# Gate and up products of experts 1 to 15 as couples of 64-row tiles, two weight pairs held at a time

## The reference

```
gate, idx = lax.top_k(aff.T, cap)                  # cap = 64 tokens of each sequence
xs = xf[idx]                                       # (16 experts, 64, 1024)
hid = jax.nn.silu(jnp.einsum('ecd,edf->ecf', xs, w_gate)) * jnp.einsum('ecd,edf->ecf', xs, w_up)
out = jnp.einsum('ecf,efd->ecd', hid, w_down) * gate[..., None]
y = zeros.at[idx.reshape(-1)].add(out.reshape(-1, D))
```

## Time and profile before

| | us |
|---|---|
| median of three runs (1526.59 to 1527.58) | 1526.74 |
| span of the profiled execution | 1525.3 |
| TensorE products busy in it | 1511.1 |
| TensorE weight loads busy in it | 1222.7 |
| VectorE busy | 1312.2 |
| ScalarE busy | 1215.8 |
| GpSimd busy | 333.7 |
| mean traffic with HBM | 324 GB/s |

### The profile page before, as it was taken

The page is one execution under the profiler, slowest core; times in us unless marked ns, Lnnn a source line. Parts: engine busy times, 40 slices in busy tenths (PEclk is TensorE's granted clock), DMA queues, the critical chain, the costliest instruction groups (busy, mean ns, idle before and its releaser), DMA issues.

```text
span 1525.3 us, 22267 instructions
## 1 busy us (share of the span) xinstructions
PE 1511.1 (99%) x7854; PEld 1222.7 (80%) x7854; DVE 1312.2 (86%) x1415; ACT 1215.8 (80%) x1435; POOL 333.7 (22%) x154
## 2 busy tenths in 40 slices
PE   9999999999999999999999999999999999999997
PEld 7888878888873787888888888888888888888886
DVE  7684786685766799999999999999999999999988
ACT  6453556344454689999999999999999999999997
POOL 0000001000012232242322423233242322420103
PEclk9999999999999999999999999999999999999999
DMA  9533547333476999999999999999999999999998
GB/s 347 182 136 127 159 139 278 109 125 98 138 240 224 395 420 395 405 394 415 398 404 403 398 408 391 399 406 406 404 393 408 399 402 403 397 411 386 391 387 353
DMA packets 156407, 498.60 MB, mean 327 GB/s; under 512 B 10880, under 2 KB 36608, under 8 KB 156352
## 3 DMA queue, kind: packets, MB, share of 16 engines
q1 hardware_dynamic: 144624, 461.54, 77.3%
q0 software_dynamic: 9280, 31.07, 6.7%
q10 hardware_dynamic: 2448, 5.25, 1.3%
HBM read 473.70 MB, written 20.97 MB: 324 GB/s over the span
## 4 chain that ended last, share of the span: by engine, by line
PE 92%; ACT 3%; DVE 2%; DMA 1%; issue 1%; SPq 0%; POOLq 0%; POOL 0%; DVEq 0%; ACTq 0%
PE ps L2063 78%; PE ps L2111 4%; PE ps L2118 2%; PE ps L2222 2%; PE ps L2162 1%; ACT w_high L1229 1%; PE ps L2380 1%; PE ps L2168 1%; DVE w_rest L1380 1%; DMA u_rows<-arena 1%; ACT arena L1200 1%; DMA raw<-w_qkv 1%; PE ps L2662 0%; PE ps L2376 0%; PE ps L2398 0%
## 5 line engine op out<-in xcount | busy, mean ns | idle before, releaser
L1380 DVE TENSOR_TENSOR w_rest<-raw,w_high 128x2048 fp32r<-128x2048 f32 x212 | 478.0, 2283 | 42.3 <-ACT w_high L1229 25.2
L1229 ACT CAST w_high<-raw 128x2048 fp32r<-128x2048 f32 x184 | 352.1, 1915 | 17.3 <-PE ps L2063 14.3
L2063 PE MATMUL ps<-w_high,xt_high 128*128 128x512 f32 x984 | 304.9, 390 | 2.3 <-DVE ht_rest L1896 1.8
L2063 PE MATMUL ps<-w_rest,xt_high 128*128 128x512 f32 x984 | 304.3, 389 | 0.0
L2063 PE MATMUL ps<-w_high,xt_rest 128*128 128x512 f32 x984 | 304.3, 389 | 0.0
L2063 PEld LDWEIGHTS ps<-w_high,xt_high 128*128 128x128 f32 x984 | 184.4, 188 | 42.6 <-issue 3.0
L1380 DVE TENSOR_TENSOR w_rest<-early,w_high 128x2048 fp32r<-128x2048 f32 x90 | 204.4, 2286 | 13.7 <-ACT w_high L1229 13.7
L2063 PEld LDWEIGHTS ps<-w_high,xt_rest 128*128 128x128 f32 x984 | 184.7, 188 | 38.4
L2063 PEld LDWEIGHTS ps<-w_rest,xt_high 128*128 128x128 f32 x984 | 184.7, 188 | 38.3
L1380 DVE TENSOR_TENSOR w_rest<-raw_more,w_high 128x2048 fp32r<-128x2048 f32 x92 | 206.0, 2273 | 5.4 <-ACT w_high L1229 5.4
L1200 ACT COPY arena<-arena 32x256 f32<-32x256 f32 x464 | 187.4, 404 | 10.8
(11 more groups left out here) (317 smaller groups left out, 2278.2 us busy)
## 6 DMA issues: line engine op xcount, KB each, us to landing
raw<-w_down SPq DMA_DIRECT2D x64, 1024.0 KB, 8.5
raw<-w_gate SPq DMA_DIRECT2D x62, 1024.0 KB, 8.6
raw<-w_up SPq DMA_DIRECT2D x62, 1024.0 KB, 8.9
raw_more<-w_down SPq DMA_DIRECT2D x32, 1024.0 KB
early<-w_down SPq DMA_DIRECT2D x32, 1024.0 KB, 7.9
raw_more<-w_gate SPq DMA_DIRECT2D x31, 1024.0 KB
raw_more<-w_up SPq DMA_DIRECT2D x31, 1024.0 KB
early<-w_gate SPq DMA_DIRECT2D x31, 1024.0 KB, 9.2
```

What stands on the lines that cost most here:

```text
L1229: nc.scalar.copy(w_high[:, i % SLOTS, :], src).then_inc(high_done, 1)
L1380: nc.vector.tensor_tensor(w_rest[:, j, :], src, w_high[:, j, :].bitcast(F32), ALU.subtract).then_inc(rest_done, 1)
L2063: done = nc.tensor.matmul(out, lhs, rhs, start=start and part == 0, stop=stop and part == 2)
```

## The change

In `gate_up` each product over 128 rows becomes two products over 64 rows, one on partitions 0 to 63 and one on 64 to 127, issued one behind the other. Such a couple works on two weight pairs at a time, the gate pair and the up pair of the same features (a group; a call has four). The six steps of a run are three parts times two chunks. In run 0 the lower rows take the gate pair into bank 0 and the upper rows the up pair into bank 2; run 1 does the same for banks 1 and 3; in runs 2 and 3 the roles are swapped (lower rows up, upper rows gate), so that each bank gets both halves of the rows. TensorE waits for its own earlier runs (`run_done`, new, and `pair_used`) so that the two tiles never write one bank at once. `pair_used` is raised by two at the end of the fourth run. Both pairs' `rest_done`, and all waits for the banks, now stand ahead of the group. The number of columns that stream is the same per couple as per product before (512), and the number of products is doubled. The semaphore `k_high` is merged into `q_high`. The queues of ScalarE, VectorE, SyncE and GpSimd for the experts are unchanged.

```
--- before.py
+++ after.py
@@ -162,6 +162,8 @@
 THIRD_BANKS = (5, 7)
 FOURTH_BANKS = (6, 7)
 LIST_BANKS = (4, 6)
+RUNS = 4
+SIGNALS = RUNS - 1
 TABLE_BANKS = ((4, 4), (6, 4))
 ROW_BANKS = (4, 6)
 
@@ -324,7 +326,6 @@
         wq_in = [sem(f"wq_in{part}") for part in range(Q_PARTS - 1)]
         wk_in = sem("wk_in")
         q_high, q_rest = sem("q_high"), sem("q_rest")
-        k_high = sem("k_high")
         diag_done = sem("diag_done")
         rstd_mm = sem("rstd_mm")
         rstd_t_done = sem("rstd_t_done")
@@ -412,6 +413,7 @@
         third_silu_done, third_hid_done = sem("third_silu_done"), sem("third_hid_done")
         first_xt_done = sem("first_xt_done")
         xt_mm, xth_done, xtr_done = sem("xt_mm"), sem("xth_done"), sem("xtr_done")
+        run_done = sem("run_done")
         silu_done, hid_done = sem("silu_done"), sem("hid_done")
         ht_mm, hth_done, htr_done = sem("ht_mm"), sem("hth_done"), sem("htr_done")
         last_in = sem("last_in")
@@ -1107,7 +1109,7 @@
                 act.wait_ge(xt_in[kc], 16)
                 nc.scalar.activation(ut_high[:, kc * T:(kc + 1) * T], xt_raw[:, kc, :], ACT.Copy,
                                      scale=g_col[:, kc:kc + 1]).then_inc(uth_done, 1)
-            first_high(1, 0, K_PARTS, wk_in, k_high)
+            first_high(1, 0, K_PARTS, wk_in, q_high)
             first_high(1, 1, K_PARTS, raw_in[1], high_done)
             x_squares(0)
             first_root(0)
@@ -1789,7 +1791,7 @@
                     else:
                         first_rest(0, part, Q_PARTS, high_done, 1, rest_done)
                 split_x(0, kc, kc + 1)
-            first_rest(1, 0, K_PARTS, k_high, 1, q_rest)
+            first_rest(1, 0, K_PARTS, q_high, Q_PARTS, q_rest)
             first_rest(1, 1, K_PARTS, high_done, 2, rest_done)
             for i in (1, 3):
                 x_squares(i)
@@ -2537,18 +2539,38 @@
                 pe.wait_ge(route_done, TRUNKS + QUARTERS)
                 nc.tensor.matmul(pieces, same_lane[:, :], spread_rows[:, :, :].rearrange("p t n -> p (t n)"), start=True, stop=True).then_inc(route_mm, 1)
 
-            def gate_up(e, lo, *banks_free):
-                for i in range(GU_PAIRS):
-                    if i < len(banks_free):
-                        pe.wait_ge(*banks_free[i])
-                    j = (lo + i) % SLOTS
-                    pe.wait_ge(rest_done, SLOTS * body_q(e, lo + i) + j + 1)
-                    for k in range(2):
-                        kc = 2 * (i // 2) + k
-                        at = slice(kc * P, (kc + 1) * P)
-                        last = products([(bank(2 * (i % 2) + n), xt_high[:, at], xt_rest[:, at], *w(j, k * HALF + n * BANK, BANK),
-                                          kc == 0, kc == KC - 1) for n in range(2)])
-                    last.then_inc(pair_used, 1)
+            def run(runs):
+
+                lower, upper = slice(0, P // 2), slice(P // 2, P)
+                for step in range(2 * 3):
+                    for on, (out, what, column, pair, first, last, kc_first) in ((lower, runs[0]), (upper, runs[1])):
+                        k, part = step // 3, step % 3
+                        at, cols = slice((kc_first + k) * P, (kc_first + k + 1) * P), slice(k * HALF + column, k * HALF + column + BANK)
+                        x = xt_rest if part == 2 else xt_high
+                        weights = w_rest if part == 1 else w_high
+                        mm = nc.tensor.matmul(out, x[on, at], weights[on, pair, cols], start=first and step == 0, stop=last and step == 5)
+                return mm
+
+            def gate_up(e, lo, number, *banks_free):
+
+                for wait in banks_free:
+                    pe.wait_ge(*wait)
+                for i in range(0, GU_PAIRS, 2):
+                    for ii in (i, i + 1):
+                        pe.wait_ge(rest_done, SLOTS * body_q(e, lo + ii) + (lo + ii) % SLOTS + 1)
+                    slots = [(lo + i) % SLOTS, (lo + i + 1) % SLOTS]
+                    for r in range(RUNS):
+                        before = SIGNALS * (GU_PAIRS // 2 * number + i // 2)
+                        if r >= 2:
+                            pe.wait_ge(run_done, before + r - 1)
+                        elif r and i:
+                            pe.wait_ge(pair_used, pairs_before(e) + lo + i)
+                        elif i:
+                            pe.wait_ge(run_done, before)
+                        what, n, opened = r // 2, r % 2, r < 2
+                        last = run([(bank(2 * of + n), of, n * BANK, slots[of], i == 0 and opened, i == GU_PAIRS - 2 and not opened, i)
+                                       for of in (what, 1 - what)])
+                        last.then_inc(*((run_done, 1) if r < SIGNALS else (pair_used, 2)))
 
             def down(s, h, e, lo, first=0, end=D_PAIRS, lhs=None):
 
@@ -2622,26 +2644,26 @@
             pe.wait_ge(ys_done, 1)
             down(0, 0, 0, 8, 0, 2)
             first_hidden_t(1, 6)
-            gate_up(0, 10, (xtr_done, 3))
+            gate_up(0, 10, 0, (xtr_done, 3))
             down(0, 0, 0, 16, 2, 3)
-            gate_up(0, 19, (silu_done, 3), (hid_done, 3))
+            gate_up(0, 19, 1, (silu_done, 3), (hid_done, 3))
             down(0, 0, 0, 24, 3, 4)
             down(1, 1, 0, 28)
             products_read(1)
             with pe.Fori(1, E - 2) as f:
-                gate_up(f, 8, (xtr_done, f + 3), (htr_done, 2 * f + 1))
+                gate_up(f, 8, 2 * f, (xtr_done, f + 3), (htr_done, 2 * f + 1))
                 pe.wait_ge(ys_done, f + 1)
                 down(2 * f, 0, f, 16, 0, 1)
-                gate_up(f, 17, (silu_done, 2 * f + 3), (hid_done, 2 * f + 3))
+                gate_up(f, 17, 2 * f + 1, (silu_done, 2 * f + 3), (hid_done, 2 * f + 3))
                 down(2 * f, 0, f, 24, 1, 4)
                 products_read(f + 1)
                 down(2 * f + 1, 1, f, 28)
-            gate_up(E - 2, 8, (xtr_done, E + 1), (htr_done, 2 * E - 3))
+            gate_up(E - 2, 8, 2 * E - 4, (xtr_done, E + 1), (htr_done, 2 * E - 3))
             pe.wait_ge(ys_done, E - 1)
             down(2 * E - 4, 0, E - 2, 16)
             down(2 * E - 3, 1, E - 2, 20)
             pe.wait_ge(hid_done, 2 * E - 1)
-            gate_up(E - 1, 0)
+            gate_up(E - 1, 0, 2 * E - 3)
             pe.wait_ge(ys_done, E)
             down(2 * E - 2, 0, E - 1, 8, 0, 2)
             pe.wait_ge(hid_done, 2 * E)
```

## The result

The changed kernel takes 1732.34 us (median of four runs, 1727.13 to 1733.40) against 1526.66 us before: 1.134 times as long, with a 95% interval of 1.1327 to 1.1353. The profiled execution has a span of 1731.6 us, 206.3 more than before. The forecast was 1708, with 1660 to 1760 around it.

A forecast was written before the change was run, and what follows sets the result against it. TensorE was taken as the bound, with ScalarE and VectorE within 4%. Thirteen repetitions at 12.3 us more plus 21.6 elsewhere gave 182 us, on the 1525.3 span 1707, so 1708 us as median; range 1660 to 1760.

The forecast's parts named there:

- The bound: Expert loop: TensorE sets the time, 65.28 us a repetition; ScalarE busy 63.1 us and VectorE 62.6 us of it.
- The term that decides: Holding two weight pairs per group: refill path 7.1 us, cover 5.4 us; repetition 77.6 us against 65.3.
- The eight waits: TensorE waits in one loop repetition, followed through three engine queues: 0.1 to 2.9 us each, 11.4 in all.
- Expert 0's part: The two calls of expert 0, by the same reckoning as the loop: 10.9 us more.
- The couples: gate_up's 64-row product pairs: 224 ns instead of 226.6, 2880 couples, minus 7 us, ends 0 and minus 31.
- The lower end, 216 ns: Fastest spacing allowed for a couple of 512 columns, from the kernel's last sixteen products; sum 172 us instead of 182.
- Tiles in and out: Entering and leaving 64-row tiles in each call: 0.1 us in, 0.23 out, 10 us for 30 calls.
- The clock: Rival: 1.2 GHz for the group behind the 2.6 and 2.9 us waits, 150 us in all, 1860; chance 0.06.
- a sign of being wrong: Listed for the loop: granted clock below 1.00, a repetition under 66 us, or couples at 453 ns.
- the filling is hidden: Rival: couples win and the casts and subtractions for a group hide under the other group, 1505 us; chance 0.05.
- couples run in sequence: Rival: 512-column couples do not run together, 453 ns each, 653 us more, 2180; chance 0.02.
- the waits are half of what was reckoned: Rival: queued work catches up, so the waits cost 91 us, 1560 to 1660; chance 0.06.

The follow-up runs named there:

- hold_full: The changed kernel with each couple replaced by one product over 128 rows, waits and release kept; 1748.42 us, 1.144 times before.
- swap_full: swap_tiles with full-height products in the same order, waits and releases; 1585.20 us, 1.0378 times before.
- need_rel: The kernel before, no tiles, with weight pairs both needed in twos and given back in twos, bank waits unchanged; 1717.93 us, ratio 1.1247.
- narrow: The kernel before with gate_up products over 256 columns instead of 512, twice as many; 1563.35 us, ratio 1.0239.
- swap_tiles: The changed kernel with each couple on one weight pair, banks exchanged two runs later, pairs held for less; 1586.02 us, ratio 1.038.
- need_only: The kernel before, no tiles, with TensorE waiting for both pairs of a group ahead of the first; 1569.39 us, ratio 1.0280.
- keep_clock_10: The changed kernel with 10 products of 128 columns into an unused bank ahead of each call's opening waits; 1723.65 us, ratio 1.1296.

## Why the prediction was right, and where it was off

**The bound.** "TensorE sets the time and two engines are within 4% of doing so" was right, and so was what followed: the time came back as idle time on three engines, with the busy time of ScalarE and VectorE unchanged. TensorE's span less its busy time grew by 150 us (164.4 against 14.2), as forecast.

**The term that decides: right.** Path 7.1 us against a cover of 5.4: the rows bear it out (7.0 from the first cast on, where the prediction has 6.9), and hold_full, swap_full and need_rel show the same cause without tiles. The repetition was put at 77.6 and took 78.4; 12.3 us more against 13.1. Of the 0.8 that are missing, 0.5 are the couples (192 at 226.6 instead of 224 ns). The eight waits came to 11.4 us by the reckoning (its entries add up to 11.5) and to 10.4 in the brackets, which count from modelled ends; from one start to the next each of the seven is some 0.16 longer (a last product's end, 0.39 behind its start, lies that much behind the next start), 11.5 in all. Single ones are off by up to 0.5, either way, and it is in part luck that they cancel. Expert 0's part was put at 10.9 and took 14.4, with low clock in it; expert 14's at 5.6 and took 4.2; the end at 3.7 and took 3.4.

**The couples: size wrong.** I took 224 ns from the scores and got 226.6, the upper end. The step that failed is reading 10 ns above streaming in the scores (248 columns, 64 rows) as something that 64-row tiles bring. The narrow products show a fixed 13.3 at full height; why the scores have only 10 there stays open. The lower end, 216 ns, was the spacing of plain float32 products of 256 columns, another kind of product, and no run shows it for a couple. The term is 0 and not minus 7 us. The rule of the Trainium skill (TensorE: Matmul & The Clock Gate, Part 3, "The mechanism"), by which a load hides only behind products of another row group, would have made this the place of a gain. Before and after, loads of 188 and 189 ns disappear in a spacing of 227 ns, to the same rows and to others, so the trace does not bear it out for these products. The other page of the Trainium skill (TensorEngine Tiling (Array Packing), "The Problem"), that tiles are for contractions of 64 or less, agrees with the runs.

**Tiles in and out: right in size, wrong in place.** 0.33 us a call was in the sum, 10 us for 30 calls. On the way out it is to be seen behind the last couple of a call:

```profile
854.11 0.40 PE L2551 MATMUL ps<-w_high,xt_rest 64*128 64x512 f32 x2
854.44 0.73 PE L2065 MATMUL ps<-w_high,ht_high 128*128 128x512 f32 x2
855.01 0.62 PE L2065 MATMUL ps<-w_rest,ht_high 128*128 128x512 f32 x2
```

The starts are 0.33 and then 0.57 us (for two products) apart, where a spacing of 227 ns gives 0.23 and 0.45: 0.22 us a call, as reckoned. On the way in TensorE waits in the loop anyway. And yet swap_tiles and swap_full differ by 0.8 us, and the ordinary repetitions of hold_full and of the changed kernel are both 78.4 us: the next wait takes it up. "Where TensorE waits on entering anyway, less" was the right half of the sentence.

**The clock: a rival that came true in part.** I gave 0.06 to a fall behind both long waits of every repetition, 150 us. It came in 4 of 13 repetitions, for 3.7 us each in those that can be compared. A granted clock below 1.00 in the loop was named as a sign of being wrong, and that sign came: 0.94 in those repetitions. It does not touch the reckoning of the waits, which holds in the nine others. The row I held against it, a wait of 1.82 us without a fall, was shorter than the 2.9 in question, and a single one; waits of 1.86 to 1.91 us had no fall in most repetitions of need_only and keep_clock_10 and had one in others, so one row could not settle it. It should have been a term of the sum with ends 0 and 48 us (13 times 3.7), not a rival of its own that happens or doesn't. Of the 24 us by which 1708 is low, 11.1 are this in three repetitions, some 4 the couples (186 against 182 in the prediction's own sum), and 3.5 expert 0's part.

**The rivals.** That the filling is hidden (1505 us) needed the path to be under 5.4 us; it is 7.0. That couples run in sequence (2180) is refuted by the spacing. That the waits are half of what was reckoned is refuted by the waits.

**What stays open:** which repetitions get the low clock. The same waits are in all of them, and with full products in their place twice as many repetitions had it as with couples (8 and 4, in one profile of each). It is no accident of one execution: the mean clock was 0.970 to 0.974 in all four runs of hold_full and 0.986 to 0.990 in all four of the changed kernel. The cause was not looked for further. No kernel here beats the kernel before. With couples at the price of full products, no order of them has anything to win on TensorE.

## What to carry to other kernels

Before putting two buffers of a pipeline into one step, compare for one buffer the path from its release to its next use with the work that covers it, at the new release and the new need. Here both ends moved by one pair, each alone was worth 3 to 4%, and together 12%. Where, as here, an engine is busy for 96% of a repetition, little of the time that it sits waiting for a release comes back. And before splitting a product into tiles that run side by side, see what a product costs above its columns: if that is paid per couple too and the contraction already fills the rows, there is nothing to split for.

## What the runs showed of the hardware that was not expected

- A product of the split format has a fixed cost of 13.3 ns above its columns at 2.4 GHz (226.6 ns at 512, 120 at 256), each with a weight load of its own. A couple of 64-row products of 512 columns costs the same 226.6 ns in all.
- The same waits brought the clock to its 1.2 GHz level in some repetitions and not in others: 2.6 and 2.9 us with shorter ones between in 4 of 13 repetitions (the changed kernel, 3.7 us longer then), one of 1.9 us, the only one of a repetition, in 3 of 13 (need_only, 1.6 us longer). In need_rel, with no wait over 2.4 us, every repetition had a stretch. Ten products (2.4 us) inside the waits that open the calls made these stretches rare.
- A float32 product of 128 by 128 by 128 took about 0.22 us, a spacing as large as that of 512 columns in the split format.
